# Odd layer's attention output by channel: values stationary, turned probabilities moving, scaled by GpSimd before they are turned

## What is computed

```python
def forgetting_attention(q, k, v, log_f):
    cum = jnp.cumsum(log_f.astype(jnp.float32), axis=1).transpose(0, 2, 1)
    for blk in range(s_len // Q_BLOCK):              # 2 blocks of 128 queries
        q0, q1 = blk * Q_BLOCK, (blk + 1) * Q_BLOCK
        logits = jnp.einsum("bqhd,bkhd->bhqk", q[:, q0:q1], k[:, :q1]) * scale
        logits = logits + cum[:, :, q0:q1, None] - cum[:, :, None, :q1]
        probs = jax.nn.softmax(jnp.where(mask[None, None], logits, -1e30), axis=-1)
        outs.append(jnp.einsum("bhqk,bkhd->bqhd", probs, v[:, :q1]))

def conformer_conv(p_d, dw_w, dw_b, cn_g, cn_b):
    h = p_d[..., :D_D] * jax.nn.sigmoid(p_d[..., D_D:])
    h = layer_norm(causal_dwconv(h, dw_w) + dw_b, cn_g, cn_b)
    return jax.nn.silu(h)

def odd_mixer(...):
    ...
    return jnp.concatenate([y_c, y_d], axis=-1) @ w_out
```

## Time and profile before

| | |
|---|---|
| median of 3 runs | 1144.40 us (1144.31 to 1144.77) |
| profiled execution, own time | 1144.23 us |
| its span | 1142.4 us |
| TensorE busy | 1133.1 us, 99% of the span |
| VectorE, ScalarE, GpSimd busy | 785.3, 601.8, 40.5 us |
| odd attention, first logits matmul to first matmul of the output projection | 320.61 to 340.25 us |

### The profile page before, as it was taken

The page is one execution under the profiler, slowest core; times in us unless marked ns, Lnnn a source line. Parts: engine busy times, 40 slices in busy tenths (PEclk is TensorE's granted clock), DMA queues, the critical chain, the costliest instruction groups (busy, mean ns, idle before and its releaser), DMA issues.

```text
span 1142.4 us, 18767 instructions
## 1 busy us (share of the span) xinstructions
PE 1133.1 (99%) x6990; PEld 931.6 (82%) x6990; DVE 785.3 (69%) x1170; ACT 601.8 (53%) x894; POOL 40.5 (4%) x80
## 2 busy tenths in 40 slices
PE   9999999999999999999999999999999999999998
PEld 8988888888878888888788788888887878888886
DVE  6898665558888866555788876656467887765641
ACT  5456454425964554452566665545356676554530
POOL 0110000000000000000000100000000010000000
PEclk9999999999999999999999999999999999999999
DMA  9857876645724787765575269776448534977740
GB/s 350 282 169 230 275 214 218 214 154 194 237 88 147 226 268 215 221 207 156 184 245 186 61 205 280 213 219 217 162 152 290 149 101 143 295 215 216 222 164 37
DMA packets 190025, 229.06 MB, mean 201 GB/s; under 512 B 16600, under 2 KB 133632, under 8 KB 189952
## 3 DMA queue, kind: packets, MB, share of 16 engines
q1 hardware_dynamic: 184272, 215.89, 60.0%
q10 hardware_dynamic: 5328, 11.91, 3.2%
q0 software_dynamic: 352, 0.30, 0.2%
HBM read 213.33 MB, written 1.06 MB: 188 GB/s over the span
## 4 chain that ended last, share of the span: by engine, by line
PE 50%; issue 1%; DVE 1%; ACT 0%; POOL 0%; POOLq 0%; DVEq 0%
PE ps L689 15%; PE ps L691 15%; PE ps L690 15%; PE ps L1050 1%; PE ps L1108 1%; PE ps L1133 0%; PE ps L863 0%; PE ps L1080 0%; PE ps L1100 0%; PE ps L1097 0%; DVE w_lo L1700 0%; PE ps L882 0%; PE ps L909 0%; PE ps L908 0%; PE ps L1079 0%
## 5 line engine op out<-in xcount | busy, mean ns | idle before, releaser
L1700 DVE TENSOR_TENSOR w_lo<-raw,w_hi 128x1024 fp32r<-128x1024 f32 x376 | 444.4, 1216 | 117.8 <-ACT w_hi L1291 114.7
L1291 ACT ACTIVATE w_hi<-raw 128x1024 fp32r<-128x1024 f32 x377 | 383.3, 1056 | 152.7 <-DMA raw<-w_down 32.9
L689 PE MATMUL ps<-w_hi,a_hi 128*128 128x512 f32 x980 | 384.5, 392 | 1.0 <-DVE w_lo L1700 1.0
L691 PE MATMUL ps<-w_hi,a_lo 128*128 128x512 f32 x980 | 381.5, 389 | 0.0
L690 PE MATMUL ps<-w_lo,a_hi 128*128 128x512 f32 x980 | 381.4, 389 | 0.0
L689 PEld LDWEIGHTS ps<-w_hi,a_hi 128*128 128x128 f32 x980 | 183.9, 188 | 40.8 <-DVE w_lo L1700 2.0
L691 PEld LDWEIGHTS ps<-w_hi,a_lo 128*128 128x128 f32 x980 | 184.0, 188 | 38.7
L690 PEld LDWEIGHTS ps<-w_lo,a_hi 128*128 128x128 f32 x980 | 184.0, 188 | 37.3
L689 PE MATMUL ps<-w_hi,h_hi 128*128 128x512 f32 x480 | 188.3, 392 | 0.2
L690 PE MATMUL ps<-w_lo,h_hi 128*128 128x512 f32 x480 | 186.9, 389 | 0.0
L691 PE MATMUL ps<-w_hi,h_lo 128*128 128x512 f32 x480 | 186.8, 389 | 0.0
(11 more groups left out here) (227 smaller groups left out, 767.7 us busy)
## 6 DMA issues: line engine op xcount, KB each, us to landing
raw<-ffn_w_in SPq DMA_DIRECT2D x176, 256.0 KB, 3.9
raw<-w_in SPq DMA_DIRECT2D x96, 256.0 KB, 3.8
raw<-ffn_w_out SPq DMA_DIRECT2D x88, 256.0 KB, 3.1
raw<-w_gate SPq DMA_DIRECT2D x88, 256.0 KB, 3.3
raw<-w_up SPq DMA_DIRECT2D x88, 256.0 KB, 4.3
raw<-w_down SPq DMA_DIRECT2D x88, 256.0 KB, 3.2
moved<-turned SPq DMA_DIRECT2D x176, 64.0 KB, 2.6
raw<-od_w_in SPq DMA_DIRECT2D x40, 256.0 KB, 3.6
```

The lines of the kernel that those rows point to most:

```text
L689: nc.tensor.matmul(ps[:, bank, :], hi, wh, start=first, stop=False)
L691: return nc.tensor.matmul(ps[:, bank, :], lo, wh, start=False, stop=last)
L1291: nc.scalar.activation(w_hi[:, v.slot, :], raw[:, v.slot, :], ACT.Copy).then_inc(w_high, 1)
L1700: V.tensor_tensor(w_lo[:, v.slot, :], raw[:, v.slot, :], w_hi[:, v.slot, :].bitcast(F32), ALU.subtract).then_inc(w_low, 1)
```

## The change

In the odd layer the product with the values is made the other way round. A pair of heads is taken together (`pair_values`): the values (128 keys by 64 channels) are stationary, in one of two strips of 64 columns, and 128 turned probabilities move; the result has the channels on the partitions, as the projection wants it, and is split right from PSUM (`split_pairs`). The result need no longer be turned, and it can no longer be scaled behind the product by a factor per partition. So the probabilities are scaled before they are turned: VectorE takes the reciprocals of one head's two sums (`head_share`), and GpSimd multiplies the head's 128x128 and 128x256 probabilities in place by them (`even_out`), in two instructions. `head_turn` waits for that (`evened`) where it waited for the exponential (`weighed`). The order of the lists changes with it: three quads stand ahead of the first head's turn, ScalarE takes the exponentials of four heads ahead of the first copy and of the heads of a pair together, VectorE's 22 taps are spread otherwise. The hybrid layers (2 and 3) keep their code; their stages are only counted from their own first layer.

On TensorE:

```diff
             def head_turn(l, h):
-                pe.wait_ge(weighed.sem, weighed.at(l, h))
+                ready = evened if LAYERS[l] == "odd" else weighed
+                pe.wait_ge(ready.sem, ready.at(l, h))
...
                 pair_logits(l, 2)
+                tap_quads_of(range(4, 7))
                 for j in range(HEADS // 2):
                     head_turn(l, 2 * j)
                     head_turn(l, 2 * j + 1)
...
                     if j == 1:
                         pair_logits(l, 3)
+                    else:
+                        first = {0: 7, 2: 10, 3: 13}[j]
+                        tap_quads_of(range(first, first + 3))
...
+                    pair_values(l, j)
+
+            def pair_values(l, j):
+
+                for h in (2 * j, 2 * j + 1):
+                    pe.wait_ge(p_out(l, h).sem, p_out(l, h).at(l, h // 2))
+                bank, col = (0, 2)[j // 2], SEQ * (j % 2)
+                for first, key, start, stop in ((0, 0, True, True), (P, 0, True, False), (P, 1, False, True)):
+                    for i in range(2):
+                        rows_i, at = slice(HD * i, HD * (i + 1)), first + P * key
+                        v = p_v[:, key, HD * (2 * j + i):HD * (2 * j + i + 1)]
+                        mm = nc.tensor.matmul(ps[rows_i, bank, col + first:col + first + P], v, probsT[:, i, at:at + P],
+                                              start=start, stop=stop)
+                        if stop and first:
+                            mm.then_inc(attended.sem, 1)
...
             def odd_rest():
                 attention(1)
-                turn_y(1, shared, 0)
                 pe.wait_ge(o_conv.sem, o_conv.at(1, 0))
...
                 pe.wait_ge(y_low.sem, y_low.at(1, 0))
-                out_units(1, range(4), 0)
+                out_units(1, range(2), 0)
+                pe.wait_ge(y_low.sem, y_low.at(1, 1))
+                out_units(1, range(2, 4), 0)
```

On ScalarE:

```diff
             def attention(l):
-                weights(l, 0)
-                weights(l, 1)
+                for h in range(4):
+                    weights(l, h)
                 for j in range(HEADS // 2):
-                    if 2 * j + 2 < HEADS:
-                        weights(l, 2 * j + 2)
                     turned_weights(l, 2 * j)
                     turned_weights(l, 2 * j + 1)
-                    if 2 * j + 3 < HEADS:
-                        weights(l, 2 * j + 3)
+                    if j < 2:
+                        weights(l, 2 * j + 4)
+                        weights(l, 2 * j + 5)
+                    if j == 2:
+                        split_pairs(0)
+
+            def split_pairs(i):
+
+                act.wait_ge(attended.sem, attended.at(1, 4 * i + 3))
+                nc.scalar.activation(h_hi[:, 2 * i:2 * i + 2, :], by_block((0, 2)[i]), ACT.Copy).then_inc(y_high.sem, 1)
```

On VectorE:

```diff
             def attention(l):
...
-                for j in range(HEADS // 2):
-                    head_lows(l, 2 * j)
-                    head_lows(l, 2 * j + 1)
-                    convolve((0, 7, 7, 8)[j])
+                for h in range(4):
+                    head_lows(l, h)
+                head_share(l, 0)
+                head_share(l, 1)
+                convolve(3)
+                head_share(l, 2)
+                convolve(1)
+                head_share(l, 3)
+                head_lows(l, 4)
+                head_lows(l, 5)
+                convolve(3)
+                head_share(l, 4)
+                convolve(2)
+                head_share(l, 5)
+                convolve(2)
+                head_lows(l, 6)
+                head_lows(l, 7)
+                convolve(1)
+                head_share(l, 6)
+                convolve(1)
+                head_share(l, 7)
+                convolve(9)
+
+            def head_share(l, h):
+
+                dve.wait_ge(weighed.sem, weighed.at(l, h))
+                V.reciprocal(share_of[:, :, h], total[:, :, h]).then_inc(shares.sem, 1)
```

On GpSimd, where `odd_rest`'s square roots stand behind it:

```diff
+            def even_out(l, h):
+
+                if h:
+                    pool.wait_ge(evened.sem, evened.at(l, h - 1))
+                pool.wait_ge(shares.sem, shares.at(l, h))
+                at = h % N_PROBS
+                chain.step(nc.gpsimd.tensor_scalar(probs[:, at, 0:P], probs[:, at, 0:P], share_of[:, 0, h:h + 1], None, ALU.mult))
+                chain.settle()
+                nc.gpsimd.tensor_scalar(probs[:, at, P:3 * P], probs[:, at, P:3 * P], share_of[:, 1, h:h + 1], None,
+                                        ALU.mult).then_inc(evened.sem, 1)
```

41 lines of the change are left out of this document (21 added, 20 removed).

## The result

The changed kernel takes 1147.95 us (median of 9 runs, 1147.27 to 1148.5), the kernel before 1144.65 in the same session (9 runs, 1144.31 to 1145.89). The ratio is 1.0027 with a 95% interval of 1.0019 to 1.0036: slower by 3.3 us, where I had forecast 1143.6 with a range up to 1146.7. The profiled execution took 1147.82, its span is 1146.0.

What follows compares the result with a forecast made beforehand. TensorE, busy 1133.1 of 1142.4 us, was taken as the bound. Its 19.64 us stretch became 17.7 of work plus 0.1, 0.3 and 0.6 of waiting; taking the later waypoint sum, 0.8 us less: 1143.6 us, range 1142.3 to 1146.7.

Steps and rivals of the forecast that it cites:

- GpSimd's price: GpSimd's two scalings a head take 0.30 and 0.40 us, 0.86 with gaps; ends 0.19 each, or 0.40 and 0.61.
- as a rate it isn't the bound: Eight heads cost GpSimd 6.9 us in a stretch of 15, so its rate does not limit the kernel.
- GpSimd is the bound: Rival: every turn waits for reciprocal and two scalings; at 0.5 and 0.8 us, 1146.7 to 1147.2; 11% slower by the bound.
- Its threshold: In the GpSimd rival: the gain is gone from a head's pair of about 1.0 us on; 2.3 us slower wants 1.2.
- TensorE's list: From first logits to output projection, 19.64 us loses 0.93, 3.57 and 0.20; 14.9 us of logits, quads and turns stay.
- Values by channel at 0.70 a pair: TensorE's new products with the values take 0.70 us a pair, 2.8 for all four; lower end 0.64.
- The end of 1.4: Upper end for a pair's values on TensorE: 1.4 us if two strips of 64 did not run side by side.
- Contention: GpSimd's scalings push VectorE's taps back by 0.16 or 0.26 us each time, 0.7 us before head 6's logits.
- The reciprocal: VectorE's reciprocal of two columns costs between 0.05 and 0.25 us; 0.15 taken, 0.9 for six.
- The waits: TensorE waits 0.1 us at most at the first turns, 0.3 for head 5's scaling, 0.6 at pair 2's values.
- The last tap: VectorE's convolution ends at 338.1, needed by 338.4: 0.3 us of cover where there were 3.1.
- three signs of a wrong prediction: A 256-column scaling over 0.6 us, turns waiting at each pair, or the last tap ending past 339.

Runs made afterwards that it cites:

- e9_copy: Changed kernel with GpSimd's two scalings a head replaced by in-place copies of the same columns (weights stay unscaled): 1143.64 us, ratio 0.9991.
- e3_half: Changed kernel with GpSimd scaling only 64 of the 128 and 128 of the 256 columns of each head: 1144.95 us, ratio 1.0003.
- e1_unscaled: Changed kernel with GpSimd's two scalings a head left out, turns waiting for the exponentials as before the change: 1143.71 us, ratio 0.9992.
- e12_before_beside: Kernel before the change, with GpSimd doing 16 scalings on a tile of its own and nobody waiting for them: 1144.54 us, ratio 1.0001.
- e2_no_taps: Changed kernel with all but three of the layer's 62 VectorE taps left out (one left in the stretch): 1146.1 us, ratio 1.0013.
- e11_spread: Changed kernel, reordered, ScalarE scaling odd heads' 256 columns, no waits inside GpSimd, two TensorE tap groups moved; nothing left out: 1143.46 us, ratio 0.9991.
- e10_constant: Changed kernel with GpSimd multiplying by the constant 0.5 instead of a number for each partition: 1145.56 us in its one run.
- e7_no_gap: Changed kernel with GpSimd's scalings no longer waiting for its own previous one; nothing left out: 1146.3 us, ratio 1.0016.

## Why the prediction was wrong

**The step that failed is GpSimd's price**: "At the copy's rate, (1.04 - 0.19) / 1024 = 0.83 ns a column, the two instructions of a head take 0.30 and 0.40", and then "I take the copy's". The scaling costs 2.5 ns a column and 0.28 us, so 0.60 and 0.92 us, two and 2.3 times what I took. My upper end, twice the copy's rate (0.40 and 0.61), did not reach it either, because it had no row behind it: the page showed no GpSimd arithmetic over many columns. Two kinds of rows of the kernel before did warn, and I passed them over (line, operation, shapes and count | busy us in sum, mean ns of one | idle time before):

```profile
L2384 POOL TENSOR_TENSOR stat<-stat 128x4 f32<-128x4 f32 x4 | 4.1, 1016 | 0.3
L2384 POOL TENSOR_TENSOR stat<-stat 128x1 f32<-128x1 f32 x6 | 3.3, 556 | 0.5
L2398 POOL TENSOR_SCALAR stat<-stat 128x1 f32<-128x1 f32 x7 | 2.1, 301 | 372.1 <-ACT squares L1338 372.1
```

L2384 (in the earlier trace rows with four columns) is a power: three columns more cost 0.46 us, 0.15 a column, so an operation's price on this engine can lie far from a copy's. L2398 is a TENSOR_SCALAR with a number for each partition, as the scaling is, and took 0.30 us for one column, near the fixed part of 0.28, where I had taken 0.19 from one with constants.

With the price the conclusion "as a rate it isn't the bound" falls. A head costs GpSimd 1.71 us undisturbed and 1.94 as it ran, eight of them 15.5 us, and by the estimate above a train of 11.4 would have cost nothing and one of 12.3 the whole gain. e9_copy shows it directly: with a copy in the scaling's place, the same waits and the same order, the stretch is 18.75 us where the forecast had 18.84. That it is met so closely is luck, as the errors below show.

**The rival that came true** is "GpSimd is the bound", which I gave 11% for a loss over the bound. Its mechanism was right to the row: the turns wait for the chain of reciprocal and two scalings. With 0.5 and 0.8 us it put the projection at 342.5 to 343; measured, with 0.60 and 0.92, it came 22.85 us behind the first logits, on that clock 343.46. It counted 0.4 us a head for taps in progress; measured, the stretching is 1.94 - 1.71 = 0.23 a head. With the measured pair of 1.52 us its sum would have given 344.3, so here the contention was counted too high. Its threshold, a pair of about 1.0 us undisturbed, agrees with e3_half: 0.44 + 0.60 us, and the gain is gone. Its other one, 1.2 us for a loss of 2.3, is a slip: its own sum gives that loss at 0.5 + 0.8 = 1.3 us. The Trainium skill, page "GPSIMD Engine Reference", section "Elementwise — side-by-side cycle accounting", gives about 2.6 cycles an element for two inputs and 1.03 for bodies of one or two operations, at 1.2 GHz an estimate of 2.2 and 0.9 ns. The copy's slope here, (402 - 288) / 128 = 0.9 ns, agrees with the second; a multiplication by one scalar, at 2.5 ns, lies beyond the first, and the measurement decides.

**The other steps.**

- *TensorE's list.* "14.9 us of logits, quads and turns stay" is right to 0.2: e9_copy's 18.75 less four pairs of 0.80 and the wait of 0.47 is 15.1. In the changed kernel itself it is 22.85 - 3.22 - 3.69 = 15.9, for a wait between two turns also ends their overlap: six transposes step in 0.80 us when together, 0.55 and 0.48 when a wait parts them.
- *Values by channel at 0.70 a pair* was too cheap: 0.80, so 0.4 us over four pairs. The end of 1.4, for strips of 64 that do not run side by side, is excluded.
- *Contention.* I put 0.7 us on VectorE before head 6's logits. In the changed kernel the 11 taps before them took 1.26 + 0.54 + 1.27 + 0.86 + 1.02 = 4.95 us, against 4.70 in e1_unscaled: 0.25. In e9_copy, which ran at the price that I had taken, they took 5.26: 0.56. Over all 22 it was 10.26 in the changed kernel against 9.28, 1.0 us, over half of it in the last nine. GpSimd's own loss to the taps, which stood only in a rival, was the larger half: its 16 instructions took 14.1 us where 8 x 1.52 = 12.2 are undisturbed. e12_before_beside shows that contention alone costs nothing in the kernel before, where nobody waits for GpSimd and VectorE has slack; e2_no_taps shows that it is worth 1.6 us once GpSimd is the bound.
- *The reciprocal*, 0.15 us taken: the next instruction starts 0.08 behind it, a little cheaper.
- *The waits* of 0.1 at head 1 and 0.3 at head 5 do not occur in e9_copy; that of 0.6 at pair 2's values is there with 0.47 (e9_copy) and 0.42 (e1_unscaled). These errors, 0.5 us too much, and the values and the list, 0.4 and 0.2 too little, cancelled.
- *The last tap* was forecast 17.5 us behind the first logits and ended 17.1 behind them in e9_copy; in the changed kernel 20.25, pulled along by the late turns, and still ahead of TensorE's need.

My three signs of a wrong prediction all showed: a scaling of 256 columns over 0.6 us, waiting turns in each pair, the last tap past 339.

## What to carry to other kernels

A price taken from one operation of an engine need not hold for another on the same engine: where the trace has no row of the very operation and a serial chain of eight hangs on it, the range must reach to several times the nearest row, and the rival in which that engine sets the pace deserves a chance of its own size. Look also at how far two operations of that engine already differ in the trace. Compare an engine's time per round with the round of the engine that waits, and not with the stretch as a whole: GpSimd took 15.5 us where, by the estimate, 11.4 would have cost nothing. When an idle engine is given work in a chain, give it only what fits its pace and share the rest: here (e11_spread) the sharing with ScalarE, no waits inside GpSimd, and small shifts of the orders together turned a loss of 3.3 us into a gain of about 1, whose interval reaches zero; what each of them is worth there was not measured.

## What the runs showed of the hardware that I had not expected

- GpSimd's multiplication of fp32 columns by a scalar costs 0.28 us and 2.5 ns a column (442, 602, 922 ns for 64, 128, 256), a copy in place 0.9 ns a column (288 and 402 ns for 128 and 256); a constant instead of a scalar for each partition saves 0.07 us an instruction and nothing a column (e10_constant, one run). Why the multiplication costs more than the copy no run shows.
- Where GpSimd meets a train of VectorE's taps, which read two tiles, GpSimd's scalings lose more than VectorE: in e12_before_beside one head's two scalings went from 1.63 to up to 2.34 us and eight heads lost 2.9 us, while 22 taps lost 0.69 us in all. With the shorter copies of e9_copy the losses are about even, 0.9 and 0.75 us. The Trainium skill, page "SBUF — State Buffer", section "Who interferes with whom", calls it an exclusive lock. The traces agree in that a scaling of 0.92 us took up to 1.54 beside taps.
- A wait of GpSimd for its own last scaling costs 0.08 to 0.12 us; without it the next starts where the last ends (e7_no_gap).
- VectorE scales 128x256 in 0.35 us, with the next instruction 0.27 behind its start, against GpSimd's 0.92.
